# First layer norm by token tiles, ScalarE's UP loop written out, and turns parted by fill units

## The reference

```python
mod = silu(c) @ w_mod + b_mod
shift1, scale1, gate1, shift2, scale2, gate2 = split(mod, 6)
h = x * (1 + scale1) + shift1
proj = h @ w_in + b_in               # queries, keys, values of branches a and b, gates
o_a = windowed_attention(...)        # 8 heads, 2 key heads, rotary positions
o_b = global_attention(...)          # the same, with normed queries and keys
y = (g_a * (o_a @ w_branch_a) + g_b * (o_b @ w_branch_b)) @ w_out
x = layer_norm(ALPHA * x + gate1 * y, ln1_g, ln1_b)
h = x * (1 + scale2) + shift2
u = conv3(h @ w_up) + conv_b         # 2 x 2816 columns, three taps along the tokens
y = (silu(u_gate) * u_val) @ w_down
x = layer_norm(ALPHA * x + gate2 * y, ln2_g, ln2_b)
```

## Time and profile before

| what | value |
|---|---|
| median of 3 runs | 986.14 us (985.43 to 986.46) |
| the profiled execution's own time | 985.43 us |
| its span (first to last instruction) | 983.8 us |
| PE busy | 926.7 us (94%) |
| DVE busy | 741.1 us (75%) |
| ACT busy | 551.0 us (56%) |
| POOL busy | 165.3 us (17%) |
| mean granted TensorE clock | 0.987 of full |

### The profile page before, as it was taken

One profiled execution on the slowest core, in us unless ns is written; L12 is line 12 of the kernel. 1 busy time (PEld: TensorE's weight loads), 2 busy tenths in 40 slices (PEclk: granted clock), 3 DMA queues, 4 the chain that ended last, 5 costly groups with the idle time before them and its releaser, 6 DMA issues.

```text
span 983.8 us, 13860 instructions
## 1 busy us (share of the span) xinstructions
PE 926.7 (94%) x4700; PEld 742.9 (76%) x4700; DVE 741.1 (75%) x1058; ACT 551.0 (56%) x818; POOL 165.3 (17%) x250
## 2 busy tenths in 40 slices
PE   6999999998999799999999999999999699999996
PEld 5787787776767587888888887666677588777785
DVE  5887466877666778887679797865767979998946
ACT  6557655474666455555333345757753467776633
POOL 7000000216300000110012001640000313333300
PEclk9999999998999999999999999999999899999999
DMA  8675544765643255887598755223235255556571
GB/s 256 222 243 153 166 130 146 256 240 162 184 136 97 87 182 193 261 270 258 171 344 306 238 172 187 80 68 95 86 130 192 65 181 164 168 169 211 174 235 43
DMA packets 99746, 175.11 MB, mean 178 GB/s; under 512 B 8252, under 2 KB 36444, under 8 KB 99692
## 3 DMA queue, kind: packets, MB, share of 16 engines
q1 hardware_dynamic: 92460, 148.87, 47.5%
q0 software_dynamic: 7184, 25.50, 7.6%
q10 hardware_dynamic: 48, 0.04, 0.0%
HBM read 173.33 MB, written 1.05 MB: 177 GB/s over the span
## 4 chain that ended last, share of the span: by engine, by line
PE 59%; DVE 14%; issue 11%; ACT 8%; POOL 4%; DMA 2%; SPq 0%; POOLq 0%; ACTq 0%; DVEq 0%
PE acc L747 47%; DVE wlo L1774 4%; ACT whi L1323 2%; PE turned L1216 1%; PE turned L783 1%; PE turned L840 1%; PE scores L1205 1%; POOL act_lo L716 1%; DMA raw<-in_w_mem_kv 1%; POOL work L713 1%; POOL conv L713 1%; DMA raw<-in_w_down 1%; PE scores L986 1%; DVE turn L1829 1%; DVE soft L2422 1%
## 5 line engine op out<-in xcount | busy, mean ns | idle before, releaser
L1774 DVE TENSOR_TENSOR wlo<-raw,whi 128x1024 fp32r<-128x1024 f32 (+2 forms) x270 | 345.1, 1301 | 108.3 <-ACT whi L1323 99.1
L1323 ACT CAST whi<-raw 128x1024 fp32r<-128x1024 f32 (+2 forms) x270 | 273.3, 1030 | 179.8 <-PE acc L747 146.7
L747 PE MATMUL acc<-whi,lta_lo 128*128 128x512 f32 (+2 forms) x576 | 230.7, 401 | 8.3 <-DVE lta_lo L1814 6.8
L747 PE MATMUL acc<-wlo,lta_hi 128*128 128x512 f32 (+2 forms) x576 | 222.8, 387 | 0.0
L747 PE MATMUL acc<-whi,lta_hi 128*128 128x512 f32 (+2 forms) x576 | 222.6, 387 | 0.0
L747 PEld LDWEIGHTS acc<-whi,lta_lo 128*128 128x128 f32 x576 | 108.8, 189 | 46.8 <-issue 15.1
L747 PEld LDWEIGHTS acc<-wlo,lta_hi 128*128 128x128 f32 x576 | 108.6, 189 | 22.4
L747 PEld LDWEIGHTS acc<-whi,lta_hi 128*128 128x128 f32 x576 | 109.0, 189 | 19.2
L747 PE MATMUL acc<-whi,ltb_lo 128*128 128x512 f32 (+1 forms) x272 | 108.9, 400 | 8.0 <-DVE wlo L1774 4.8
L642 POOL DMA_DIRECT2D wm<-in_w_mod x48 | 34.4, 719 | 464.0 <-DVEq L1874 266.9
L747 PE MATMUL acc<-whi,ltb_hi 128*128 128x512 f32 (+1 forms) x272 | 105.7, 389 | 0.0
(11 more groups left out here) (349 smaller groups left out, 1354.2 us busy)
## 6 DMA issues: line engine op xcount, KB each, us to landing
raw<-in_w_in SPq DMA_DIRECT2D x88, 512.0 KB, 4.0
wm<-in_w_mod POOLq DMA_DIRECT2D x48, 512.0 KB, 5.7
raw<-in_w_up SPq DMA_DIRECT2D x88, 256.0 KB, 3.1
raw<-in_w_up SPq DMA_DIRECT2D x32, 512.0 KB, 4.6
raw<-in_w_down SPq DMA_DIRECT2D x32, 512.0 KB, 5.1
raw<-in_w_down SPq DMA_DIRECT2D x44, 256.0 KB, 3.1
raw<-in_w_mem_kv SPq DMA_DIRECT2D x8, 512.0 KB, 5.5
raw<-in_w_o SPq DMA_DIRECT2D x8, 512.0 KB, 4.5
```

What stands on the lines that cost most here:

```text
L747: ins = pe.matmul(acc[s][:, t, 0:n], lhs[part][:, kt0 + kk, tok], w[:, u % RING, kk, 0:n], start=(k == 0 and kk == 0 and j == 0), stop=(la ...
L1323: act.copy(whi[:, s, :, 0:n], raw[:, s, :, 0:n]).then_inc(hi_ready, 1)
L1774: dve.tensor_tensor(wlo[:, s, :, 0:n], raw[:, s, :, 0:n], whi[:, s, :, 0:n].bitcast(F32), ALU.subtract)\
```

## The change

- **First norm.** DVE takes mean and variance of a half tile by `bn_stats` and joins them by `bn_aggr`; ACT keeps only the root. The first token tile is normed and turned (`turn_x3`) before the last half unit of OUT1, a bank now holds four channel tiles of one token tile, ACT does the scale and shift of three of the four banks (four Identity activations of 128x128 each) besides the high cast, and UP0 runs first on token tile 0, four units, then on token tile 1.
- **Gate rows.** No diagonals and no `ones`: PE turns the column of `modc`, broadcast over 128 columns, as a transpose. The row of gate2 is turned in UP0 and read out by ACT.
- **Turns.** Branch a: queries before unit 1 of IN2, keys before unit 3. Branch b and gate1: one bank before `fill_rest`, the other in `after`.
- **ACT's UP loop** is written out as ten panels; PE, DVE, POOL and SP keep their loops.
- **Residual.** POOL's two passes over x are gone. DVE does them in DN0 as eight 128x512 instructions, two after each of four splits; the row vectors of the second norm are loaded at unit 4 of DN1 instead of after UP10.
- **Second norm** by half tiles, with `bn_stats`, and four stores of 256 KB in place of two of 512 KB.

The core of the diff:

```diff
-    out += g("x2", 4) + g("kA", 2) + g("qA", 2)
+    out += g("x2", 4) + g("qA", 2) + g("kA", 2)
...
-    out += g("ym", 4) + g("gate2", 2) + g("x3", 4)
+    out += g("ym", 4) + g("x3", 4)[:2] + g("gate2", 2) + g("x3", 4)[2:]
...
+                    if name == "DN1" and k == RING:
+                        sp.wait_ge(ev("x3_residual"), 1)
+                        for i, v in enumerate(("ln2_g_2", "ln2_b_2")):
+                            sp.dma_start(lnrow[:, i], a[v].partition_broadcast(P)).then_inc(ev("ln2_landed"), 16)
...
-            pool.wait_ge(ev("ln1_landed"), 32)
-            b, k = T_USE["x3.3"]
-            pool.wait_ge(t_full[b], k + 1)
-            order.done(pool.tensor_tensor(x[:], x[:], lnrow[:, 0].unsqueeze(1).broadcast_to([P, T, D]), ALU.mult))
-            pool.tensor_tensor(x[:], x[:], lnrow[:, 1].unsqueeze(1).broadcast_to([P, T, D]), ALU.add)\
-                .then_inc(ev("x3_residual"), 1)
...
-                if k == 3:
+                if k == 1:
+                    turn_queries(0)
+                elif k == 3:
                     turn_keys(0)
-                    turn_queries(0)
...
-                        ins = pe.matmul(bank[:, P * j:P * j + P], ones[:], diag[:, 4 * g + j, :], start=True, stop=True)
+                        c = first + 4 * g + j
+                        ins = pe.transpose(bank[:, P * j:P * j + P], modc[:, c:c + 1].broadcast_to([P, P]), ident[:])
...
+            def ab_rest(p):
+                if p > 0:
+                    ab_turn(p - 1, 0)
+                ab_fill(p, (1,))
...
-            tokens_in_turn("OUT1", lta)
-            gate_rows("gate2")
-            turn_tokens("x3", x, ready="x3_ready", after=2)
+            for t in range(T):
+                for k in range(RING):
+                    if t == T - 1 and k == RING - 1:
+                        turn_x3(0)
+                    unit("OUT1", k, lta, tokens=(t,), announce=(t == 0 and k == RING - 1))
+            for k in range(RING):
+                if k == RING - 1:
+                    gate_rows("gate2")
+                    turn_x3(1)
+                lt_wait("x3", k // 2)
+                unit("UP0", k, ltb, tokens=(0,))
+            for k in range(RING):
+                lt_wait("x3", 2 + k // 2)
+                unit("UP0", k, ltb, tokens=(1,))
...
-            panel("UP0", ltb, new="x3")
...
+            u0 = PLAN.unit["UP0"] - AHEAD
+            ahead(u0 + 1)
+            root("ln1", 0)
+            ahead(u0 + 2)
+            x3_turned(0, 0)
+            ahead(u0 + 3)
+            x3_turned(0, 1)
+            ahead(u0 + 4)
+            root("ln1", 1)
+            gate_row_out("gate2")
+            x3_turned(1, 0)
+            x3_turned(1, 1)
...
-            with act.Fori(0, 5) as i:
-                for c in (1, 2):
-                    for k in range(4):
-                        split(u0 + 4 * (c - 1) + k + AHEAD, i, 8, 64)
-                        if k == 1:
-                            conv_of(c - 1, i)
-                    upv_out(c, i)
-                    conv_hi(c - 1, i)
+            for c in range(1, FF2 // 256):
+                for k in range(KT // UNIT):
+                    ahead(PLAN.unit[f"UP{c}"] + k + 1)
+                    if k == 1:
+                        conv_of(c - 1)
+                upv_out(c)
+                conv_hi(c - 1)
...
+            for t in range(T):
+                for g in range(2):
+                    part = slice(COLS * g, COLS * g + COLS)
+                    for i, op in enumerate((ALU.mult, ALU.add)):
+                        ahead(PLAN.unit["DN0"] + 5 + 2 * t + g)
+                        done(dve.tensor_tensor(x[:, t, part], x[:, t, part], lnrow[:, i, part], op))
+            dve.sem_inc(ev("x3_residual"), 1)
+            first_half("gate2", "DN")
```

More of the change, by code:

```diff
@@ L689, in _ @@
             pool.wait_ge(ev("qA_normed"), 1)
-            b, k = T_USE["qA.1"]
+            b, k = T_USE["kA.1"]
             pool.wait_ge(t_full[b], k + 1)
@@ L1636, in _ @@
             lt_act("x2", lta, (2, 3))
-            ahead(PLAN.unit["IN3"])
             def gate2_sigmoid(n):
@@ L1657, in queries_out @@
                     t_out(f"{('qA', 'qB')[br]}.{g}", qT[br][:, 2 * g:2 * g + 2, :].rearrange("p a b -> p (a b)"))
+            ahead(PLAN.unit["IN2"] + 1)
+            queries_out(0)
+            ahead(PLAN.unit["IN3"])
             keys_out(0)
-            queries_out(0)
             def ab_exps(i, slot, row, bank):
@@ L1755, in _ @@
             ahead(PLAN.units)
-            variance("ln2", PLAN.units)
+            act.activation(stat[:, 0, 8:9], one_col[:], ACT.Sqrt)
+            for t in range(T):
+                root("ln2", t)
         @block.vector
@@ L2402, in norm_sums @@
                     done(dve.tensor_reduce(s, square, AX.X, ALU.add))
-            def diagonals(name, first):
-                for j in range(KT):
-                    ins = dve.tensor_scalar(diag[:, j, :], ident[:], modc[:, first + j:first + j + 1], None, ALU.mult)
-                done(ins)
-                dve.sem_inc(ev(f"{name}_diag"), 1)
             done(dve.memset(stat[:, 3, :], 1.0))
@@ L2495, in _, with residual @@
                 lt_dve("ym", lta, groups=(2 * c, 2 * c + 1))
-            def residual_sums(gate, src, g, t):
+            def residual(src, g, t):
                 part = slice(COLS * g, COLS * g + COLS)
@@ L2505, in residual_sums, with moments, mean_of, spread_of @@
                     done(ins)
-                done(dve.scalar_tensor_tensor(x[:, t, part], x[:, t, part], ALPHA, work[:, t, part], ALU.mult,
-                                              ALU.add, accum_out=stat[:, 1, 8 + 2 * g + t:9 + 2 * g + t]))
-            def layer_norm(gate, name, src, pos, scaled):
+                done(dve.scalar_tensor_tensor(x[:, t, part], x[:, t, part], ALPHA, work[:, t, part], ALU.mult, ALU.add))
+            def moments(g, t):
+                done(dve.bn_stats(stat[:, 4 + t, 6 * g:6 * g + 6], x[:, t, COLS * g:COLS * g + COLS]))
+            def mean_of(t):
+                return stat[:, 1, 2 + 2 * t:3 + 2 * t]
+            def spread_of(name, t):
+                v = stat[:, 1, 3 + 2 * t:4 + 2 * t]
+                done(dve.bn_aggr(stat[:, 1, 2 + 2 * t:4 + 2 * t], stat[:, 4 + t, 0:12]))
+                dve.tensor_scalar(v, v, 1.0, LN_EPS, ALU.mult, ALU.add).then_inc(ev(f"{name}_var"), 1)
+            def inverse_spread(name, t):
+                v = stat[:, 1, 3 + 2 * t:4 + 2 * t]
+                dve.wait_ge(ev(f"{name}_std"), t + 1)
+                done(dve.reciprocal(v, v))
+                return v
+            def first_half(gate, src):
                 panel_wait(f"{src}0")
@@ L2514, in layer_norm @@
                     dve.wait_ge(t_free[b], k + 2)
+                residual(src, 0, 0)
+                ahead(last_unit(f"{src}1") + 1 - AHEAD)
+                residual(src, 0, 1)
                 for t in range(T):
[L2516 to L2530 removed]
@@ L2552, in _, with normalized @@
-            layer_norm("gate1", "ln1", "OUT", PLAN.unit["UP0"], ln1_scaled)
-            lt_dve("x3", ltb, x3c[:, 0:8], x3c[:, 8:16])
+                    moments(0, t)
+            def normalized(t):
+                spread_of("ln1", t)
+                v = inverse_spread("ln1", t)
+                for half in (slice(0, COLS), slice(COLS, D)):
+                    dve.tensor_scalar(x[:, t, half], x[:, t, half], mean_of(t), v, ALU.subtract, ALU.mult)\
+                       .then_inc(ev("x3_ready"), 1)
@@ new lines, in x3_low @@
+            def x3_low(t, g):
+                n = 2 * t + g
+                dve.wait_ge(lt_hi, lt_done("x3", n))
+                part = slice(P * t, P * t + P)
+                dve.tensor_tensor(ltb[1][:, 4 * g:4 * g + 4, part], turn[:, n % 2].rearrange("p (j s) -> p j s", j=4),
+                                  ltb[0][:, 4 * g:4 * g + 4, part].bitcast(F32), ALU.subtract).then_inc(lt_ready, 1)
+            first_half("gate1", "OUT")
+            dve.wait_ge(ev("OUT1_first_tokens"), 1)
+            residual("OUT", 1, 0)
@@ new lines, in _ @@
+            moments(1, 0)
+            normalized(0)
+            u0 = PLAN.unit["UP0"] - AHEAD
+            ahead(u0 + 2)
+            x3_low(0, 0)
+            dve.wait_ge(unit_used, RING + last_unit("OUT1") + 1)
+            residual("OUT", 1, 1)
+            ahead(u0 + 3)
+            x3_low(0, 1)
+            moments(1, 1)
+            normalized(1)
+            ahead(u0 + 4)
+            b, k = T_USE["x3.3"]
+            dve.wait_ge(lt_ready, lt_done("x3", 1))
+            dve.wait_ge(t_full[b], k + 1)
@@ L2556, in taps @@
+            for j in range(4):
+                c, part = 4 + j, slice(P * j, P * j + P)
+                ins = dve.tensor_scalar(turn[:, 1, part], tb[b][:, part], x3c[:, c:c + 1], x3c[:, 8 + c:9 + c],
+                                        ALU.mult, ALU.add)
+            ins.then_inc(t_free[b], 1)
+            for g in range(2):
+                x3_low(1, g)
             def taps(c, i=None):
```

152 lines of the change are left out of this document (67 added, 85 removed).

## The result

The changed kernel takes **970.6 us** (median of 4 runs, 969.7 to 971.1) against 986.3 for the kernel before in the same session (4 runs, 985.4 to 987.1): ratio 0.985, 95% interval 0.9835 to 0.9859. The forecast was 969.9. The profiled execution has a span of 969.0 us at a mean clock of 0.989.

A forecast was written before the change was run, and what follows sets the result against it. The prediction took PE to bound the kernel, its waits mostly on DVE. Its terms, -10.2 - 3.9 - 2.5 + 0.4 = -16.2, took 986.14 to 969.9 us, with a range of 964.0 to 976.0.

The forecast's parts named there:

- First norm and UP0: Stretch from OUT1's end to UP0's end: 14.0 us of work plus 2.7 waiting replace 26.9, so -10.2 (-12.9 to -5.5).
- The four waits: PE's waits left in first norm and UP0: bank 0's low part, bank 1's, last unit's split, banks 2 and 3; 2.7 us.
- UP loop: Nine panels take 107.4 us instead of 110.8 without table loads, plus 0.5 at DN0: -3.9, between -5.2 and -1.5.
- The Trainium skill's rule: UP loop: a DVE instruction with two SBUF inputs contends with GpSimd reading SBUF; panels stay at 12.0, gaining 2.8, not 4.6.
- the wait of 0.54 has the same lateness behind it: PE's wait at the start of DN0 was laid to the UP loop's lateness and expected to go: 0.5 us.
- Turns: Turns in IN2 and AB: queries before keys, shorter gate row, banks read earlier; -2.5, between -3.8 and -0.9.
- half of the 0.96 behind the query turns: AB stage: ACT reads one query bank a half unit earlier, so its sigmoid starts earlier and 0.5 us goes.
- Residual in DN0: Eight moved DVE instructions, 5.5 us, fit into DVE's idle time in DN0, and the later row loads cost nothing: 0.
- Tail: Last matmul to the end: DVE's chain 5.6 us against 4.96, less 0.2 for the smaller store: +0.4 (-0.5 to +1.2).
- the fall of the clock in UP0: Rival: short waits in UP0 add up and the clock drops to 0.50, costing 1.7 to 3.4 us: 971.6 to 973.3; chance 0.18.
- Short chains that don't shrink: Rival: UP0 keeps waits of 7.4 us and the UP loop stays at DVE's bound: -9.1 in all, 977.0; chance 0.10.
- slow supply of ACT's code: Rival: the written-out UP loop is fetched late, delaying every panel's casts; at 2.5 us each +8.3, 994.4; chance 0.03.

The follow-up runs named there:

- u_table: The changed kernel with a small square root ahead of every second UP panel, bringing two table loads a round back: 974.6 us, ratio 0.988.
- e_few: The changed kernel with POOL's two products per UP panel cut to 16 of 256 columns, good for its time only: 967.6 us, ratio 0.982.
- u_pool: The changed kernel with POOL's two passes over x put back and DVE's eight instructions in DN0 removed: 975.7 us, ratio 0.991.
- p_loop: The kernel before with only ACT's UP loop written out: 981.9 us, ratio 0.995.
- p_pool: The kernel before with POOL's passes over x moved to DVE in DN0 and the second norm's rows loaded in DN1: 981.2 us, ratio 0.996.
- b_both: The changed kernel with the tap copy on ACT and ACT's cast of each panel's high part moved later: 969.0 us, ratio 0.983.

## Why the prediction was right

The total missed by 0.7 us, and part of that is luck: terms that missed by 0.4 to 0.5 us both ways stand in the sum, and two of them are right by pairs of errors. The terms, one by one:

- **First norm and UP0**: -10.2 forecast, -9.7 measured. The four waits were put at 0.9, 0.6, 0.5 and 0.7, sum 2.7; they are 1.15, 0.17, none and 1.09 with 0.34 at the turn of tile 1, sum 2.75. The sum is better than its parts: what was to wait behind tile 1's residual waited little, and the banks' chains were covered less. The stretch of 16.9 us up to OUT1's end is unchanged, so UP0 has 34.11 - 16.9 - 2.75 = 14.5 us of work where 14.0 was taken. That 14.0 was priced at the full clock, while the 26.9 us of before hold some 3.0 of low clock: the forecast took these 3 us as a gain without listing them, on the bet that the clock stays up, which it did. The waits of before were 8.18 and not 7.4. `bn_stats` has the 0.69 us that was guessed from the reduction.
- **UP loop**: -3.9 forecast, -4.3 measured. The nine panels came as argued, four at 11.79 and five at 11.97 (833.03 to 892.90 is 59.87), and by the cause argued: the table loads (u_table), then DVE held by POOL (e_few). The Trainium skill's rule that was weighed there (SBUF — State Buffer, Who interferes with whom) is borne out by the splits and by the low parts of u_pool, and fully blocked is what they show: each does nearly all of its work behind POOL's pass. The tap copy is held in the same way (1.28 us against 0.16), though it has one SBUF input and the sentence weighed speaks of two. The step "the wait of 0.54 has the same lateness behind it" is wrong: p_loop and p_pool show the two row loads in SP's queue. The number came out, because the change moved those too. I had put the moved loads at 0, and they were a gain of 0.5. The bound of -1.5 was a slip too: half of five waits of 0.84 is 2.1.
- **Turns**: -2.5 forecast, -2.0 measured without the clock (168.39 to 166.36). IN2 (0.9 forecast, 1.05) and the gate row (0.9, 0.83) are right. The step that failed is half of the 0.96 behind the query turns: the wait stands unchanged at 0.97. It is a wait for `probT`, so for the softmax chain, which I had left standing everywhere else. Parting in AB gives 0.15 of the 0.7 put on it.
- **Residual in DN0**: 0, right.
- **Tail**: +0.4 forecast and measured. DVE is 0.3 us late at the last tile because tile 0's scaling runs until 960.95, which I had not listed. Its chain then takes 5.66 us (960.87 to 966.53) where 5.6 was summed. What follows the last scaling shrank from 3.05 to 2.45 us, 0.6 where I had taken 0.2 for the smaller store. So the sum is right because two errors cancel. From the timelines of PE and DVE:

```profile
960.19 0.39 PE L736 MATMUL acc<-wlo,act_hi 128*128 128x512 f32 x1
...
960.87 0.68 DVE L2526 TENSOR_TENSOR work<-acc,gate_row 128x512 f32<-128x512 f32 x1
...
965.12 1.41 DVE L2670 SCALAR_TENSOR_TENSOR x_res<-work,stat,lnrow 128x512 f32<-128x512 f32 x2
```

The terms as measured, -9.7 - 4.3 - 2.0 + 0.4 = -15.6, agree with the medians (970.6 - 986.3 = -15.7). The profiled spans differ by 14.8 only, since IN0's +2.4 and the clock's -1.6 lie between those two executions.

Of the rivals, the fall of the clock in UP0 didn't come in any kernel with the new norm but u_pool, where PE waited 3.89 us; the bet that the short waits leave the clock alone held there (none is over 1.27 us), but not for the waits of 1.80 and 1.95 elsewhere. Short chains that don't shrink, and slow supply of ACT's code, are refuted by the 2.75 us of waits and by p_loop and u_table.

## What to carry to other kernels

A loop on ScalarE whose body switches between tables can pay for it in every round, here with two loads: look for table loads inside the rounds before shortening anything else. When a wait is explained, follow it to the transfer and to what stands ahead in that queue; two kernels with one part each told here what the changed kernel alone could not. When a long VectorE instruction has no reason of its own, look at what GpSimd does in the same microseconds.

## What the runs showed of the hardware

- A VectorE instruction between SBUF operands that starts beside a GpSimd pass over SBUF ends behind that pass by its own length less 0.13 us, however long the pass is: 0.69 us became 5.07 in u_pool, 1.22 became 2.3 in the UP panels, and a copy of 16 columns had 1.28 against 0.16.
- Moving steps about did not get round this: GpSimd's three passes, 4.8 us a panel, cost VectorE 3.2 us in b_both (7.89 against 4.7) and 3.2 in the changed kernel (4.53 + 1.28 against 2.44 + 0.16).
- The granted clock fell behind the same wait of 1.95 or 1.80 us in some executions and not in others, and each fall cost 0.9 to 1.7 us: it fell in 5 of 28 cases. Behind the six longer waits, of 2.44 to 4.94 us, it was at 0.50 every time. One profile of each kernel compares kernels no better than that unless the windows are read.
- Code that is the same in all kernels ended between 577.7 and 581.2 us; differences of the span under 3.5 us mean nothing before they are placed in a stage.
